# A hybrid recurrent and mixture-of-experts block on one core: gate projection started early, half of the output projection in rounded passes, routing's small matmuls and the experts' first loads in another order

## What is computed

```python
m = W_out( sigmoid(G_a h) * HGRN2(h) + sigmoid(G_b h) * [RG-LRU(conv4(h)) * gelu(.)] )
h = LayerNorm(alpha * h + m)
h = LayerNorm(alpha * h + SharedSwiGLU(h) + sum_topk w_e SwiGLU_e(h))
```

## Time and profile before

| | us |
|---|---|
| median of 3 runs | 1161.93 (1161.57 to 1162.16) |
| the profiled execution, its own time | 1162.79 |
| its span in the trace | 1160.8 |
| TensorE busy | 1118.2 (96%) |
| VectorE busy | 733.0 (63%) |
| ScalarE busy | 442.7 (38%) |
| GpSimd busy | 206.6 (18%) |

### The profile page before, as it was taken

One profiled execution on the slowest core, in us unless ns is written; L12 is line 12 of the kernel. 1 busy time (PEld: TensorE's weight loads), 2 busy tenths in 40 slices (PEclk: granted clock), 3 DMA queues, 4 the chain that ended last, 5 costly groups with the idle time before them and its releaser, 6 DMA issues.

```text
span 1160.8 us, 19340 instructions
## 1 busy us (share of the span) xinstructions
PE 1118.2 (96%) x7152; PEld 685.5 (59%) x7152; DVE 733.0 (63%) x1298; ACT 442.7 (38%) x692; POOL 206.6 (18%) x113
## 2 busy tenths in 40 slices
PE   5999999999999999999999999999999999999996
PEld 4878787878787888645533444444444444444443
DVE  8868686848486868684564555555555555555556
ACT  6756565656566656401102211221122221122214
POOL 1433342424242424200010000000000000000000
PEclk9999999999999999999999999999999999999998
DMA  6121212121212212229459999999999999999972
GB/s 238 42 110 42 111 51 100 65 88 62 89 51 101 70 81 84 99 86 418 177 225 406 419 419 419 420 419 421 419 420 420 418 415 417 411 417 416 410 325 80
DMA packets 48323, 286.70 MB, mean 247 GB/s; under 512 B 8994, under 2 KB 10530, under 8 KB 16528
## 3 DMA queue, kind: packets, MB, share of 16 engines
q1 hardware_dynamic: 43088, 272.96, 57.9%
q0 software_dynamic: 5184, 12.98, 2.9%
HBM read 287.62 MB, written 4.19 MB: 251 GB/s over the span
## 4 chain that ended last, share of the span: by engine, by line
PE 51%; DVE 2%; DMA 2%; ACT 1%; issue 0%; POOLq 0%; DVEq 0%
PE pair L1410 21%; PE pair L1473 11%; PE pair L1463 9%; PE pair L906 3%; PE pair L174 2%; PE pair L1072 2%; DMA ws_gu<-in_ws_gate_up 1%; DMA xg<-h_rows,idx 1%; PE pair L1421 1%; DVE acc L1618 0%; ACT first L1539 0%; DVE table L1295 0%; PE pair L869 0%; PE pair L1086 0%; DVE left L1296 0%
## 5 line engine op out<-in xcount | busy, mean ns | idle before, releaser
L380 PE MATMUL pair<-hT,w_parts 128*128 128x264 f32 (+1 forms) x2112 | 377.2, 338 | 2.0 <-DVE hT L642 1.6
L380 PEld LDWEIGHTS pair<-hT,w_parts 128*128 128x128 f32 x2112 | 320.6, 189 | 49.4 <-issue 4.7
L227 POOL TENSOR_TENSOR w_parts<-w_raw,w_parts 128x1024 fp32r<-128x1024 f32 x66 | 166.7, 2528 | 303.8 <-ACT w_parts L221 292.5
L1562 DVE TENSOR_TENSOR acc<-acc,pair 128x512 f32<-128x512 f32 x272 | 165.5, 679 | 38.6 <-PE pair L1463 38.6
L1410 PE MATMUL pair<-raw,xgT 128*64 128x512 f32 x768 | 170.3, 595 | 0.1
L898 POOL DMA_INDIRECT xg<-h_rows,idx x36 | 35.8, 994 | 529.8 <-DVE idx L892 461.6
L1410 PEld LDWEIGHTS pair<-raw,xgT 128*64 128x64 f32 x768 | 53.2, 137 | 116.1 <-issue 116.1
L1522 ACT ACTIVATE y_hi<-pair,small 128x512 fp32r<-128x512 f32 x70 | 48.1, 687 | 192.0 <-PE pair L1473 192.0
L1553 DVE TENSOR_TENSOR act_a<-act_s,pair 128x256 f32<-128x256 f32 x35 | 14.7, 421 | 167.9 <-ACT act_s L1515 167.9
L1515 ACT ACTIVATE act_s<-pair 128x256 f32<-128x256 f32 x35 | 13.4, 383 | 224.8 <-PE pair L1410 224.8
L1473 PE MATMUL pair<-raw,aT 128*32 128x512 f32 x768 | 87.4, 595 | 0.0
(11 more groups left out here) (296 smaller groups left out, 1289.5 us busy)
## 6 DMA issues: line engine op xcount, KB each, us to landing
raw<-in_w_gate_up SPq DMA_DIRECT2D x96, 1024.0 KB, 21.9
raw<-in_w_down SPq DMA_DIRECT2D x48, 1024.0 KB, 20.8
first<-in_w_gate_up SPq DMA_DIRECT2D x44, 1024.0 KB, 23.0
w_raw<-in_w_in SPq DMA_DIRECT2D x36, 1024.0 KB, 6.6
first<-in_w_down SPq DMA_DIRECT2D x22, 1024.0 KB, 21.2
xin<-in_x SPq DMA_DIRECT2D x4, 512.0 KB, 5.5
ws_gu<-in_ws_gate_up SPq DMA_DIRECT2D x1, 2048.0 KB, 10.2
h_rows<-acc SPq DMA_DIRECT2D x4, 512.0 KB, 14.4
```

What stands on the lines that cost most here:

```text
L227: pool.tensor_tensor(w[:, n % PARTS, 1], w_raw[:, n // 2, n % 2], w[:, n % PARTS, 0].bitcast(F32), ALU.subtract).then_inc(sem("w_lo_ready" ...
L380: last = pe.matmul(o, w[:, n % PARTS, pw, k * P:(k + 1) * P], hT[ph][:, k, of], start=(k == 0 and m == 0), stop=(k == KB - 1 and m == 2))
L1562: v.tensor_tensor(part, part, SUM[g], ALU.add).then_inc(sem("sum_free"), 1)
```

## The change

1. In the heads' loop the wait for `x_taken` and the first `HG_AHEAD` = 3 k blocks of projection GHG move ahead of the wait for xc; the other five stay where the whole was.
2. The output projection takes its blocks in the order 4, 5, 6, 0, 1, 2, 3, 7. Blocks 0 to 3 are three rounded passes from `w_parts` and from a high part (`merged_hi`, ScalarE, four copies of 512 columns behind its last head) and a low part of merged (`merged_lo`, in merged's own place, GpSimd, four subtractions of 512 columns).
3. In the second block the products of tiles 2 and 3 come first, then turns 0, 1 and 2, then the logits of three tiles with their column halves interleaved (for each k block: tile 0's two halves, tile 1's, tile 2's), then turn 3 and its logits.
4. `merged_hi` lies in ring slot 0, so that slot is loaded behind `mix_done`, and with it two chunks of `first` that were loaded ahead of it, the small iota and tok_row (256 KB).

```diff
                     last.then_inc(pe_sem["kt_done"], 1)
+                    pe.wait_ge(sem("x_taken"), j + 1)
+                    project(GHG, BF_, range(HG_AHEAD))
                     pe.wait_ge(sem("xc_ready"), j + 1)
...
                     last.then_inc(pe_sem["kv_done"], 1)
-                    pe.wait_ge(sem("x_taken"), j + 1)
-                    project(GHG, BF_).then_inc(pe_sem["hg_done"], 1)
+                    project(GHG, BF_, range(HG_AHEAD, KB)).then_inc(pe_sem["hg_done"], 1)
...
 def project_out(pe, mem, banks, t, n, j):
 
-    return pe.matmul(banks[2 * (t % 2) + n][:, :], mem["merged"][:, j, t * P:(t + 1) * P],
-                     mem["w_raw"][:, j // 2, j % 2, n * 512:(n + 1) * 512], start=(j == 0), stop=(j == HEADS - 1))
+    to, rows, cols = banks[2 * (t % 2) + n][:, :], slice(t * P, (t + 1) * P), slice(n * 512, (n + 1) * 512)
+    start, stop = j == OUT_ORDER[0], j == OUT_ORDER[-1]
+    if j >= PARTS:
+        return pe.matmul(to, mem["merged"][:, j, rows], mem["w_raw"][:, j // 2, j % 2, cols], start=start, stop=stop)
+    for m, (part, pw) in enumerate((("merged_hi", 0), ("merged_hi", 1), ("merged_lo", 0))):
+        last = pe.matmul(to, mem[part][:, j, rows], mem["w_parts"][:, j, pw, cols], start=(start and m == 0),
+                         stop=(stop and m == 2))
+    return last
...
-            for j in range(HEADS):
-                if j % 2 == 0:
-                    pe.wait_ge(sem(f"w_here_{j // 2}"), 16 * (HEADS + 1))
+            for m in range(PAIRS):
+                pe.wait_ge(sem(f"w_here_{m}"), 16 * (HEADS + 1))
+            for j in OUT_ORDER:
+                if j < PARTS:
+                    pe.wait_ge(sem("w_lo_ready"), GROUPS * HEADS + PARTS + j + 1)
...
+            act.wait_ge(sem("merged_done"), PARTS)
+            act.wait_ge(sem("u2_ready"), HEADS)
+            for j in range(PARTS):
+                act.activation(mem["merged_hi"][:, j], merged[:, j], ACT.Copy).then_inc(sem("w_hi_ready"), 1)
...
+            for j in range(PARTS):
+                pool.wait_ge(sem("w_hi_ready"), GROUPS * HEADS + PARTS - 1 + j + 1)
+                pool.tensor_tensor(mem["merged_lo"][:, j], merged[:, j], mem["merged_hi"][:, j].bitcast(F32),
+                                   ALU.subtract).then_inc(sem("w_lo_ready"), 1)
...
-        def logits(t):
-            pe.wait_ge(sem("h1T_taken"), t + 1)
+        def logits(ts):
+            pe.wait_ge(sem("h1T_taken"), ts[-1] + 1)
             for k in range(KB):
-                for of in column_halves:
...
+                for t in ts:
+                    for of in column_halves:
...
         project(2)
-        for t in range(EARLY):
+        project(3)
+        for t in range(TT - 1):
             turn(t)
-        project(3)
-        turn(2)
...
-        for t in range(TT - 1):
-            logits(t)
+        logits(range(TT - 1))
         turn(TT - 1)
-        logits(TT - 1).then_inc(sem("logits_done"), 1)
+        logits((TT - 1,)).then_inc(sem("logits_done"), 1)
...
-        for slot in range(NORM_CHUNK):
+        for slot in range(1, NORM_CHUNK):
             if slot not in (MERGED_CHUNK, MERGED_CHUNK + 1):
                 ring(slot)
+
+
+        sp.wait_ge(sem("mix_done"), TT)
+        sp.dma_start(ws_gu[:], a["ws_gate_up"]).then_inc(sem("shared_here"), 16)
+        sp.dma_start(iota[:], a["iota"]).then_inc(sem("iota_here"), 16)
+        sp.dma_start(pairs.tok_row[:], a["tok_row"]).then_inc(sem("iota_here"), 16)
+        for slot in (0, MERGED_CHUNK, MERGED_CHUNK + 1):
+            ring(slot)
         for u in range(PAIR):
             bring(2, u, 1)
-
-        sp.wait_ge(sem("mix_done"), TT)
-        sp.dma_start(ws_gu[:], a["ws_gate_up"]).then_inc(sem("shared_here"), 16)
-        for slot in (MERGED_CHUNK, MERGED_CHUNK + 1):
-            ring(slot)
```

More of the change, by code:

```diff
@@ L32 @@
 EARLY = 2
+HG_AHEAD = 3
 CHUNK = 64
@@ L65 @@
 MERGED_CHUNK, NORM_CHUNK = 4, 9
+OUT_ORDER = (4, 5, 6, 0, 1, 2, 3, 7)
 DOWN_BANK = (4, 2, 6, 4)
@@ L147, in program @@
         mem["raw"] = sb("raw", [P, RING, CHUNK_W])
-        mem["merged"] = sb("merged", [P, HEADS, T], at=raw_at + MERGED_CHUNK * CHUNK_W * 4)
+        merged_at = raw_at + MERGED_CHUNK * CHUNK_W * 4
+        mem["merged"] = sb("merged", [P, HEADS, T], at=merged_at)
+        mem["merged_lo"] = sb("merged_lo", [P, PARTS, T], F32R, at=merged_at)
+        mem["merged_hi"] = sb("merged_hi", [P, PARTS, T], F32R, at=raw_at)
         ring_end = top[0]
@@ L206, in front @@
     top[0] = after_w
-    w = sb("w_parts", [P, PARTS, 2, D], F32R)
+    w = mem["w_parts"] = sb("w_parts", [P, PARTS, 2, D], F32R)
     reset = sb("reset", [P, TA])
@@ L363, in _, with project @@
                     j = 2 * r + s
-                    def project(g, bank=None):
+                    def project(g, bank=None, ks=range(KB)):
                         n = W_ORDER.index(g)
@@ L370, in project @@
                         pe.wait_ge(sem("w_lo_ready"), GROUPS * j + n + 1)
-                        for k in range(KB):
+                        for k in ks:
                             if g == GF:
@@ L1005, in _ @@
         for t, n in ((rw, "router_w"), (rbias, "router_bias"), (before, "before"), (before2, "before2"),
-                     (count, "count"), (steps6, "steps6"), (e_col, "e_col"), (iota, "iota"),
+                     (count, "count"), (steps6, "steps6"), (e_col, "e_col"),
                      (onehot, "onehot"), (tok, "tok")):
@@ L1010, in _ @@
         sp.dma_start(ws_dn[:], a["ws_down"]).then_inc(sem("shared_here"), 16)
-        sp.dma_start(pairs.tok_row[:], a["tok_row"]).then_inc(sem("tok_row_here"), 16)
         def bring(third, u, c):
@@ L1059, in turn @@
             last.then_inc(sem("h1T_done"), 1)
-        def logits(t):
-            pe.wait_ge(sem("h1T_taken"), t + 1)
+        def logits(ts):
+            pe.wait_ge(sem("h1T_taken"), ts[-1] + 1)
             for k in range(KB):
-                for of in column_halves:
-                    last = pe.matmul(R[of, t * E:(t + 1) * E], h1T[:, k, t * P + of.start:t * P + of.stop], rw[:, k],
-                                     start=(k == 0), stop=(k == KB - 1))
+                for t in ts:
+                    for of in column_halves:
+                        last = pe.matmul(R[of, t * E:(t + 1) * E], h1T[:, k, t * P + of.start:t * P + of.stop], rw[:, k],
+                                         start=(k == 0 and t == ts[0]), stop=(k == KB - 1), skip_group_check=True)
             return last
@@ L1090, in _ @@
         project(2)
-        for t in range(EARLY):
+        project(3)
+        for t in range(TT - 1):
             turn(t)
-        project(3)
-        turn(2)
-        pe.wait_ge(sem("route_here"), 16 * 10)
+        pe.wait_ge(sem("route_here"), 16 * 9)
         pe.wait_ge(sem("mix_taken"), 3)
-        for t in range(TT - 1):
-            logits(t)
+        logits(range(TT - 1))
         turn(TT - 1)
-        logits(TT - 1).then_inc(sem("logits_done"), 1)
+        logits((TT - 1,)).then_inc(sem("logits_done"), 1)
         pe.wait_ge(sem("shared_here"), 32)
@@ L1212, in _ @@
             normed(t)
-        v.wait_ge(sem("route_here"), 16 * 10)
+        v.wait_ge(sem("route_here"), 16 * 9)
         v.wait_ge(sem("scores_ready"), 1)
@@ L1287, in _ @@
         v.wait_ge(sem("tables_done"), 1)
+        v.wait_ge(sem("iota_here"), 32)
         st(v.tensor_scalar(slot_of[:, 0:ITEMS].rearrange("p i (b t) -> p b t i", b=2), spread(pair[0]), FAR, None,
@@ L1580, in _ @@
         v.sem_inc(sem("sum_free"), ADDS)
-        v.wait_ge(sem("tok_row_here"), 16)
         pairs.build(v, 0, 3 * PAIR)
```

## The result

| | before | changed |
|---|---|---|
| median (6 runs each) | 1162.07 us | 1145.03 us (1143.05 to 1148.23) |
| the profiled execution, its own time | 1162.79 us | 1144.19 us |
| its span | 1160.8 us | 1142.2 us |
| mean granted clock of it | 0.994 | 0.997 |

The ratio is 0.9858, 95% interval 0.9844 to 0.9872: 16.5 us faster (14.9 to 18.1). The forecast was 1147.0 us in a range of 1144.0 to 1152.0; its 15.2 us lead from the profiled execution to 1147.6 and from the median of the first three runs to 1146.7, and 1147.0 was taken between them.

The account below looks back on a forecast made before the run. The prediction held that the experts' stream waits for the routing's plan, so time won ahead of it arrives whole. Its terms, 9.2 + 2.2 + 3.1 + 0.7 = 15.2 us, led to 1147.0 us, range 1144.0 to 1152.0.

Parts of the forecast that it names:

- The frame: Between the kernel's halves: the experts' loads wait for the routing's plan; routing ending x us sooner ends the kernel x sooner.
- Part 1: Heads' loop: nine gate-projection matmuls moved ahead fill TensorE's wait for xc, 9.2 us won, bounds 8.1 and 9.3.
- The state chain's margin of 0.45 us: Each head: VectorE's state chain takes 3.1 us, the 15 matmuls left behind cover 3.56, so state is ready 0.45 early.
- Part 2: Output projection: rounded passes for blocks 0 to 3 save 2.45 us in tiles 0 and 1, taken as 2.2; as much in 2 and 3.
- the strict reading: Output projection: all four GpSimd subtractions hold VectorE, and the block ends up to 2.8 us later than 509.9.
- Part 3: Second block's products, turns and logits: gain 4.2 us (2.4 from passes, 1.8 from moved turns), loss 1.1, net 3.1.
- Part 4: Loads: 3 MB fewer ahead of the shared experts' weights remove TensorE's 0.72 us wait; deferred loads cost nothing.
- The sum: Whole kernel: 9.2 + 2.2 + 3.1 + 0.7 = 15.2 us won.
- The rival of the clock: Short matmuls behind the filled wait: both low-clock stretches go as well, end 3.4 us earlier, 1144; chance 0.12.
- The rival of the turns: Row of turns and narrow logits: the clock falls there, some 8 us of work up to doubled, 1155; chance 0.05.

Follow-up runs that it names:

- run 1: Kernel before with only the x_taken wait and three k blocks of GHG moved ahead of the wait for xc: 1152.74 us, ratio 0.9922.
- run 2: Kernel before with only the new order, tile 3's product ahead of turns 0 to 2, loads as before: 1163.16 us, ratio 1.0016.
- run 3: Kernel before with run 2's order, and ring slot 0 and two chunks of `first` loaded behind `ws_gu`: 1158.93 us, ratio 0.9975.
- run 5: Changed kernel with five k blocks of GHG ahead of the wait for xc instead of three: 1154.06 us, ratio 0.9918.
- run 4: Changed kernel with all output blocks in full precision and natural order, no copies or subtractions of merged: 1149.76 us, ratio 0.9898.
- run 8: Changed kernel with run 7's order of logits and PSUM banks of its own for each tile's product: 1144.35 us, ratio 0.9835.
- run 11: Changed kernel with two k blocks of GHG ahead of the wait for xc instead of three: 1146.93 us, ratio 0.9869.
- run 7: Changed kernel with logits tile by tile and tile 3 turned before tile 2's logits: 1144.68 us, ratio 0.9844.
- run 6: Changed kernel with the logits of tiles 0 to 2 one tile after the other instead of interleaved: 1146.02 us, ratio 0.9855.

## Why the prediction was right, by its steps

- **The frame: the plan sets the start of the experts' stream, and what is won ahead of it arrives whole.** Held: 18.4 us ahead of the plan, 18.6 in all.
- **Part 1, 9.2 us.** By run 1 9.1 (6.9 to 11.2). By the two profiles it is more: from the first head's turned keys to the output projection it was 424.9 us (59.78 to 484.66), 421.8 without the 3.1 of low clock, and is 411.3 (61.40 to 472.74), so 10.4. But 1.5 of it belongs to that one execution. In the first head TensorE came early and waited 1.82 us for xc; in runs 2 and 3, whose heads are those of before, it came 2.5 to 2.7 us later and waited 0.3. The gate matmuls' row in the first head, before and in run 3, and then run 3's waits of this kind:

```profile
62.31 1.98 PE L415 MATMUL pair<-xc,lw 128*128 128x512 f32 x4 [1.82 <-DVE xc L709]
```

```profile
63.47 1.98 PE L415 MATMUL pair<-xc,lw 128*128 128x512 f32 x4 [0.26 <-DVE xc L709]
PE pair L415 <- DVE xc L709: 6.6, 8, 1.0
```

In both runs the same way is 420.2 us (run 2: without its one stretch of low clock there), 8.9 more than with part 1. That the forecast of 9.2 comes so near is partly luck, two errors against each other: the sum of 8.1 us of waits had this first head in it, where run 3 has 6.6, and what the idle rows miss was put at 0.15 us a head, where it is 0.28 by run 3 (8.9 less 6.6, over 8). Some 0.1 of that is the two gate products, which are 0.1 us longer behind a wait (1.98 against 1.88).

- **The state chain's margin of 0.45 us.** Held; run 5 shows the price on the other side of it, 0.9 us a head.
- **Part 2, 2.2 + 2.4.** By the rows of run 4 2.6 + 2.6, by its times 4.6. A group of three passes is 0.70 us where 0.7125 was forecast: by the whole 0.866 less 0.161 (2.57 over 16), and by starts 10.46 us for 15 groups (483.81 to 494.27). VectorE was held 1.8 us, within the 0 to 2.5 allowed, and its cover was just enough. The rule of the Trainium skill (SBUF — State Buffer, on its two separate sides) is borne out for the operations with two SBUF inputs, 1.58 and 1.63 us instead of 0.69. The reciprocal behind them, 3.35 us as in every other head, ran unhindered under the third and fourth subtraction, so the strict reading, all four holding VectorE, did not come.
- **Part 3, 3.1.** Gain 4.4 (4.2 said), loss 1.2 (1.1 said). What the sum did not say: part of it comes only with the moved loads. In run 2 the order alone brings 1.2 us by the rows, and nothing by the times.
- **Part 4, 0.7.** The row of 0.72 us went as said. As a price of the loads it was too small: with the new order they are worth 1.4 us by the rows (run 3 against run 2). As both came together, the sum was not hurt.
- **The sum.** By rows 8.9 + 2.6 + 4.4 - 1.2 + 0.7 = 15.4 us, forecast 15.2. The 18.4 us of the two profiles are these 15.4, 3.1 of low clock and 1.5 of the first head's wait, less the 1.6 by which the changed trace comes to the first head later. The ratio says 16.5 (14.9 to 18.1), which takes in the 15.4. Its middle is 1.1 higher; the six changed executions have a median clock of 0.996, the 43 of the kernel before beside the experiments 0.994, and at the 0.7 to 0.9 us for 0.001 given below that would be 1.4 to 1.8 us, an estimate.
- **The rival of the clock.** One profile before and one after could have told a false story: two stretches of low clock against none, 3.1 us (3.4 said). Eleven more profiles have between none and four, with and without part 1.
- **The rival of the turns.** It did not come: in none of the thirteen profiles does a stretch of low clock lie in the turns or the logits.

## What to carry to other kernels

Work ahead of a wait may be pulled forward from behind the next group only as far as two margins allow: the wait's own length, and what the pulled work covered where it stood; the rows give both, and here two blocks more cost some 7 us, one block less 0.8 by the rows, which the times can't tell from nothing. Before a reordering is priced, ask which load lands at its new end: the new order alone was worth 1.2 us by the rows and nothing by the times, and with three loads moved 2.6 by the rows and 2.9 (1.5 to 4.3) by the times. Where matmuls of several tiles are interleaved, all of them wait for the last tile's operand.

## What was unexpected of the hardware

TensorE's granted clock fell from 2.4 to 1.2 GHz for a short while in places that change from one execution to the next, none to four times in each of the thirteen profiles (the last 8 us or so, where TensorE has no more work and every profile shows a lower clock, are left out). Such a place reads as in run 1, a mean granted clock of 0.57 to 0.58 over a stretch of 4 us, and costs 1.6 us in the middle of a head (57.29 us against 55.73 in run 1), 0.8 in run 5, whose heads have a wait in them. In eight of the thirteen one stands behind TensorE's wait of some 2 us between 42 and 48 us, in three (runs 2, 8 and 11) one stands in the first matmuls, at 16 to 24 us; others are in the short matmuls of a head (in eight profiles), in the shared expert and routing (runs 4 and 7) and at the experts' start (runs 5 and 8). The changed kernel's profile and run 6 have none, though both have the wait of 2 us too. So the rows show neither that waits bring it on nor that steady work prevents it. The executions differ accordingly, with much scatter: by straight lines through the executions of run 2, of run 3 and of the kernel before beside them, 0.001 of mean clock goes with 0.7 to 0.9 us, yet run 2's fastest, 1160.08 us, had 0.992. What releases it stays open.

Four subtractions of 512 columns on GpSimd took 6.79 us, where one of 1024 takes 2.4 to 3.0. Their records (shortest, median and longest in ns, first and last start in us):

```profile
L810 POOL TENSOR_TENSOR merged_lo<-merged,merged_hi x4: 1267/1713/2224, 476.5 to 482.0; 128x512 fp32r<-128x512 f32 x4
```

The first, beside VectorE's operations with two SBUF inputs, took 2.22 us; the last, which began at 482.0 beside the reciprocal alone, took 1.27, half of a record of 1024 columns. At that size four would be 5.1 us, the 5 that I had halved. So the rest, 1.7 us, came of the company and not of the smaller size, as far as spans on GpSimd, which are rough, can say.
